# A head's retrieval in seven pieces behind seven gather steps, in place of four behind four

## The chip, the cores and the metric

One core of one Trainium2 chip runs the whole program in one launch. The metric is the device time in microseconds of one execution. Of three executions of the kernel before, the median is 2275.62 us (2271.41 to 2276.86).

## The reference, cut to what matters

One inference step of a decoder layer: 512 prompt tokens and 32 sample tokens, width 1024, float32. A mixer (a convolution branch, a dilated attention branch and gates) gives `x1`; then comes a lookup layer, PEER, with 16384 experts, and it is the lookup that the change is about:

```python
q = (hb @ w_peer_q).reshape(PEER_BLOCK, PEER_HEADS, 2, PEER_HALF)
s = jnp.einsum('thpc,hpkc->thpk', q, sub_keys)           # 8 heads x 2 halves x 128 scores
s1, i1 = lax.top_k(s[:, :, 0], PEER_TOPK)                # 16 best of each half
s2, i2 = lax.top_k(s[:, :, 1], PEER_TOPK)
cand = (s1[..., :, None] + s2[..., None, :])             # 16 x 16 sums
top_s, top_c = lax.top_k(cand, PEER_TOPK)                # 16 best sums
idx = e1 * N_KEYS + e2                                   # e1, e2: keys looked up in i1, i2 by top_c
g = softmax(top_s)
a = einsum(hb, expert_u[idx]);  out = (g * gelu(a)) @ expert_v[idx]
```

For each token and each of 8 heads, 16 experts are found ("the retrieval"), and one row of `expert_u` and one of `expert_v` is fetched for each.

## The kernel before, in words

**Tiles.** The tokens stand in five tiles: prompt tiles 0 to 3 (128 tokens each) and the sample tile, number 4 (`NT`, 32 tokens). The mixer runs in two passes, first over tiles 0, 1 and 4, then over 2 and 3.

**Gather steps.** The expert work is a row of 544 steps (`ST`), in the order of tiles 0, 1, 4, 2, 3. One step fetches 128 rows of 8 KB, u and v side by side, for 32 tokens and 4 of one head's 16 experts; a head of a prompt tile is 16 steps, a head of the sample tile 4. In each step:
- GpSimd issues the indirect DMA into one of six slots of `ring` (line 1088), after it has waited until the step six back has left its slot, and at a head's first step until the head's picks are there (`pick_ready`)
- VectorE waits for the rows and forms the 128 dot products with the tokens (line 1894; it will be called the dot)
- ScalarE applies Gelu (line 1480) and makes the weights `fold` (line 1483, from line 1476)
- TensorE multiplies them with the v halves into `acc` (line 1310) and with that frees the slot.

**The retrieval of a head** is VectorE's, but for three small things. Its four parts in the kernel before: `halves` (top 16 of both halves of the scores, by `top16`: MAX8, FIND_INDEX8, MATCH_REPLACE8, MAX8, FIND_INDEX8, lines 1794 to 1798), `candidates` (the 256 sums and their top 16, lines 1820 to 1826), `keys_named(q, 0)` (the first key of each of the 16, lines 1831 to 1837), and `experts` (the second key, then expert numbers and softmax weights, lines 1834 to 1847). ScalarE does the exponential (`head_exp`, line 1465), for which it waits until `candidates` is done; `experts` waits for it in turn. TensorE then spreads numbers and weights to 128 partitions (`spread`, line 1292), into the one bank `o` that the attention output (`O`) and the convolution (`C`) also use in turn; VectorE copies them out (`place`, lines 1859 and 1860). The scores of a head are loaded from memory by SyncE for tiles 0, 1 and 4 (`load_scores`, line 839) and are still on the chip for tiles 2 and 3.

**Where the retrieval stands.** `ITEMS` lists the 40 (tile, head) pairs by the step `at` at which each begins: a prompt head 16 steps ahead of its own first step, so at every 16th step, with the sample heads set between them, 8 steps off. `PARTS` sets part p of a head right behind the dot of step at + p, in VectorE's order. ScalarE does the exponential behind step at + 1.

**The order of everything.** A planner (`plan`) lays the mixer's work out in 508 ticks, and each engine goes through the same ticks in its own order: the tick's mixer tasks first, then gather steps up to `MARK[n]` (VectorE and ScalarE run 2 steps ahead of TensorE, GpSimd up to 6). The steps 0 to 271 are laid into the ticks of the second half of the mixer; after the last tick 272 steps are left, with nothing else beside them. This second stretch will be called the tail. `spread` and `place` stand in the second tick after the one in which VectorE passes step at + 3 (`place_picks`); in the tail `spread` stands ahead of step at + 5 of TensorE, and `place` behind the dot of step at + 7.

Of the kernel before, what the change touches and what calls it, by code (L numbers as in the profile page):

```python
# [9 lines left out]
ALU = mybir.AluOpType  # L10
# [19 lines left out]
KEYS, TOPK, PH, HALF = 128, 16, 8, 128  # L30
RMS_EPS, LN_EPS = 1e-6, 1e-5
NEG = -1.0e30
LOW = -3.0e38
# [63 lines left out]
def tile_rows(t):  # L97
    return P if t < NT else SMP
# [34 lines left out]
PH_OF = {t: p for p, some in enumerate(PAIRS) for t in some}  # L133
# [58 lines left out]
LEAD_V, LEAD_A = 2, 2  # L192
# [169 lines left out]
UNITS, TICKS, ENDS = plan()  # L362
# [32 lines left out]
START = ENDS["wq", 0, 0] + 8  # L395
# [26 lines left out]
MARK = step_marks()  # L422
# [12 lines left out]

ITEMS = item_list()
ITEM_NO = {(t, h): q for q, (_, t, h) in enumerate(ITEMS)}
PARTS = {}
for _q, (_at, _t, _h) in enumerate(ITEMS):
    for _p in range(4):  # L440
        if _at >= 0:
            PARTS.setdefault(_at + _p, []).append((_q, _p))
SCORES_AT = {ITEMS[q - 1][0] + 2 if q > 2 and (t, h) != (2, 0) else max(at - 3, 0): q for q, (at, t, h) in enumerate(ITEMS) if at >= 0}


def place_picks():

    tail = {}  # L450
    for q, (at, _, _) in enumerate(ITEMS):
        n = START if q == 0 else next((n for n in range(START, len(TICKS)) if MARK[n] + LEAD_V > at + 3), len(TICKS)) + 2
        if n < len(TICKS):
            TICKS[n].append(("P", q))
            TICKS[n].sort(key=lambda v: ORDER[v[0]])
        else:
            tail[at + 5] = q
    return tail


# [136 lines left out]
def program(nc, a, sc):  # L597
    with ExitStack() as ctx:
# [22 lines left out]
        tv, tif, caf, e12 = sb("tv", [P, 2, TOPK]), sb("tif", [P, 2, TOPK]), sb("caf", [P, 2, TOPK]), sb("e12", [P, 2, TOPK])  # L621
        ti, ca, ci = sb("ti", [P, 2, TOPK], U32), sb("ca", [P, 2, TOPK], U32), sb("ci", [P, TOPK], U32)
        cand, cv, ex = sb("cand", [P, TOPK, TOPK]), sb("cv", [P, TOPK]), sb("ex", [P, TOPK])
        nmx, exs = sb("nmx", [P, 1]), sb("exs", [P, 2])
# [39 lines left out]
        flat = ring[:, :, :].rearrange("p r d -> p (r d)")  # L664
# [43 lines left out]
        def kept_scores(t):  # L708

            return sx[:, 0:2 * PH * KEYS] if t == 2 else uT[:, :, :].rearrange("p c t -> p (c t)")[:, 0:2 * PH * KEYS]  # L710
# [750 lines left out]
        def _(eng):  # L1461
# [7 lines left out]
            def steps_upto(last):  # L1469
                for i in range(done[0], min(last, STEPS)):  # L1470
                    t, h, j, s = ST[i]
                    if j == J_ORDER[t][0] and s == 0:
                        eng.wait_ge(pick_ready, ITEM_NO[t, h] + 1)
                    if i >= 2:
                        eng.wait_ge(fold_ready, i - 1)
                    eng.activation(by_pick[:, i % 2, :], cst[:, C_FOLD:C_FOLD + SUB], ACT.Copy, scale=picks(i, 1)).then_inc(by_ready, 1)  # L1476
                    eng.wait_ge(dot_ready, i + 1)
                    if i >= 4:
                        eng.wait_ge(v_used, i - 3)
                    eng.activation(gel[:, i % 4:i % 4 + 1], dots[:, i % 4:i % 4 + 1], ACT.Gelu).then_inc(gel_ready, 1)  # L1480
                    eng.wait_ge(gel_ready, i + 1)
                    eng.wait_ge(by_ready, i + 1)
                    eng.activation(fold[:, i % 4, :], by_pick[:, i % 2, :], ACT.Copy, scale=gel[:, i % 4:i % 4 + 1]).then_inc(fold_ready, 1)  # L1483
                    for q, p in PARTS.get(i, ()):
                        if p == 1:
                            head_exp(q)
                done[0] = max(done[0], last)

# [8 lines left out]
            for n, tick in enumerate(TICKS):  # L1497
                if n == ENDS["glu", 0, 3]:
                    eng.wait_ge(rest_in, 16)
                for v in tick:  # L1500
                    if v[0] == "X0":
                        t = v[1]
# [10 lines left out]
                    elif v[0] == "XT":  # L1513
                        t, q = v[1:]
                        m = tile_rows(t)
# [236 lines left out]
        def _(eng):  # L1752
            count = [0]

            def link(ins):
                count[0] += 1
                ins.then_inc(chain, 1)
                eng.wait_ge(chain, count[0])

            def signal(ins, s, n):  # L1760
                ins.then_inc(s, 1)
                eng.wait_ge(s, n)
# [30 lines left out]
            def top16(values, index, x):  # L1793
                link(eng.max(values[:, 0:8], x))
                link(eng.max_index(index[:, 0:8], values[:, 0:8], x))  # L1795
                link(eng.match_replace(x, values[:, 0:8], x, LOW))
                link(eng.max(values[:, 8:16], x))  # L1797
                return eng.max_index(index[:, 8:16], values[:, 8:16], x)  # L1798

            def halves(q):  # L1800
                _, t, h = ITEMS[q]
                m, of = tile_rows(t), sco2
                if PH_OF[t]:
                    freed(eng, SB, s_free, ("SC", t, h // 2))
                    of = kept_scores(t)[:, 2 * KEYS * h:2 * KEYS * (h + 1)]
                elif q:
                    eng.wait_ge(sco_in, 16 * q)
                else:
                    freed(eng, SB, s_free, ("SC", 0, 0))
                    link(eng.tensor_copy(sco2[:, :], sco[:, 0, 0:2 * KEYS]))  # L1810
                for p in range(2):
                    ins = top16(tv[0:m, p, :], ti[0:m, p, :], of[0:m, KEYS * p:KEYS * (p + 1)])
                    if p:
                        signal(ins, half_done, q + 1)
                    else:
                        link(ins)

            def candidates(q):
                m = tile_rows(ITEMS[q][1])
                link(eng.tensor_copy(tif[0:m, :, :], ti[0:m, :, :]))  # L1820
                if q:
                    eng.wait_ge(o_ready, OB.no["P", q - 1] + 1)
                link(eng.tensor_tensor(cand[0:m, :, :], tv[0:m, 0, :].unsqueeze(2).to_broadcast([m, TOPK, TOPK]),
                                       tv[0:m, 1, :].unsqueeze(1).to_broadcast([m, TOPK, TOPK]), ALU.add))
                link(top16(cv[0:m, :], ci[0:m, :], cand[0:m, :, :].rearrange("p a b -> p (a b)")))
                signal(eng.tensor_scalar(nmx[0:m, :], cv[0:m, 0:1], -1.0, None, ALU.mult), top_ready, q + 1)

            def keys_named(q, p):
                m = tile_rows(ITEMS[q][1])
                if p == 0:  # L1830
                    link(eng.tensor_scalar(ca[0:m, 0, :], ci[0:m, :], 4, None, ALU.logical_shift_right))
                    link(eng.tensor_scalar(ca[0:m, 1, :], ci[0:m, :], TOPK - 1, None, ALU.bitwise_and))
                    link(eng.tensor_copy(caf[0:m, :, :], ca[0:m, :, :]))
                link(eng.tensor_tensor(cand[0:m, :, :], caf[0:m, p, :].unsqueeze(2).to_broadcast([m, TOPK, TOPK]),  # L1834
                                       cst[0:m, C_IOTA:C_IOTA + TOPK].unsqueeze(1).to_broadcast([m, TOPK, TOPK]), ALU.is_equal))
                link(eng.tensor_tensor(cand[0:m, :, :], cand[0:m, :, :], tif[0:m, p, :].unsqueeze(1).to_broadcast([m, TOPK, TOPK]), ALU.mult))  # L1836
                link(eng.tensor_reduce(e12[0:m, p, :], cand[0:m, :, :], AX, ALU.add))  # L1837

            def experts(q):
                m = tile_rows(ITEMS[q][1])  # L1840
                keys_named(q, 1)
                link(eng.scalar_tensor_tensor(out=e12[0:m, 0, :], in0=e12[0:m, 0, :], scalar=float(KEYS), in1=e12[0:m, 1, :], op0=ALU.mult, op1=ALU.add))
                own_j = cst[0:m, C_JM:C_JM + QUAD].unsqueeze(2).to_broadcast([m, QUAD, TOPK])
                link(eng.tensor_tensor(igm[0:m, :, 0, :], e12[0:m, 0:1, :].to_broadcast([m, QUAD, TOPK]), own_j, ALU.mult))
                eng.wait_ge(ex_ready, q + 1)
                link(eng.reciprocal(exs[0:m, 1:2], exs[0:m, 0:1]))
                signal(eng.scalar_tensor_tensor(out=igm[0:m, :, 1, :], in0=ex[0:m, :].unsqueeze(1).to_broadcast([m, QUAD, TOPK]), scalar=exs[0:m, 1:2], in1=own_j,
                                                op0=ALU.mult, op1=ALU.mult), ig_ready, q + 1)
# [12 lines left out]
                eng.sem_inc(o_free, 1)  # L1861

            def part(q, p):
                if p == 0:
                    halves(q)
                elif p == 1:
                    candidates(q)
                elif p == 2:
                    keys_named(q, 0)
                else:  # L1870
                    experts(q)

# [30 lines left out]
            for n, tick in enumerate(TICKS):  # L1903
# [182 lines left out]
                if n in CONV[0]:  # L2086
                    conv_upto(0, CONV[0][n])
                if START - 4 <= n < START:
                    part(0, n - START + 4)
                steps_upto(lead(n, LEAD_V))  # L2090
            steps_upto(STEPS)
            for f, (last, _, _) in enumerate(FIN):
# [65 lines left out]
```

## Time and profile before

| | |
|---|---|
| median of three runs | 2275.62 us |
| the profiled execution | 2276.75 us, span 2274.9 us |
| TensorE, VectorE, ScalarE, GpSimd busy | 71%, 65%, 38%, 33% of the span |
| indirect gathers | 544, 570.46 MB (1.049 MB each) |
| all DMA | 752.49 MB, mean 331 GB/s |
| VectorE: the dots | 544 x 1225 ns |
| GpSimd waiting for TensorE to free a slot | 878.1 us |

The span is cut into 40 slices of 56.9 us. The second half of the DMA row reads 9 in nearly every slice, the TensorE clock row falls from 9 to 5 in the 28th slice, where the mixer ends and the tail begins:

```profile
DVE  2587773114658687878887767336666765676774
PEclk9999999998899998789999999896555555555555
DMA  5333557666899989799999999999999999999998
```

A digit is a tenth of the slice's time (PEclk: of the full clock); 9 stands for 90% or more, so a 9 in the DMA row can still hide a few per cent.

### The profile page before, as it was taken

What the parts mean: (1) busy time and instruction counts of PE and PEld (TensorE: products, weight loads), DVE (VectorE), ACT (ScalarE), POOL (GpSimd) and SP (SyncE); (2) the same over time, 40 slices, a digit from 0 to 9 for tenths busy, and PEclk for the clock granted to TensorE, in tenths of its full rate; (3) what the DMA queues carried; (4) which work ended last, traced back from release to release, by engine and by line L of the source; (5) the groups of instructions that cost most, each with busy time, mean ns of one, the idle gap of its engine ahead of it and who ended that gap; (6) DMA issues with size and microseconds to landing.
All of it is one profiled execution on the core that took longest, in us unless ns stands there. A gap on an engine that the chain in (4) does not pass through costs nothing.

```text
span 2274.9 us, 33445 instructions
## 1 busy us (share of the span) xinstructions
PE 1614.9 (71%) x11548; PEld 737.8 (32%) x11548; DVE 1469.4 (65%) x3591; ACT 857.9 (38%) x2426; POOL 757.3 (33%) x713
## 2 busy tenths in 40 slices
PE   7999999996798877777778988794344343443343
PEld 3556655443343433434333433341000000000000
DVE  2587773114658687878887767336666765676774
ACT  2132243012445434544556543333333332333332
POOL 1254100001233243333533333333444343444343
PEclk9999999998899998789999999896555555555555
DMA  5333557666899989799999999999999999999998
GB/s 189 129 109 119 200 202 275 213 209 247 318 406 341 372 312 381 292 363 375 358 381 360 363 406 409 394 377 391 394 391 406 397 401 371 395 400 409 408 405 364
DMA packets 129188, 752.49 MB, mean 331 GB/s; under 512 B 16724, under 2 KB 40908, under 8 KB 51308
## 3 DMA queue, kind: packets, MB, share of 16 engines
q0 software_dynamic: 78336, 570.46, 63.7%
q1 hardware_dynamic: 50684, 179.90, 21.4%
q8 instruction: 92, 1.51, 0.3%
q14 instruction: 76, 0.62, 0.1%
HBM read 732.61 MB, written 18.54 MB: 330 GB/s over the span
## 4 chain that ended last, share of the span: by engine, by line
PE 34%; DMA 28%; DVE 24%; issue 9%; ACT 4%; POOL 1%; SPq 0%; DVEq 0%; POOLq 0%; ACTq 0%
DMA ring<-in_expert_uv,pick 25%; PE z L1156 20%; DVE ring L1894 6%; PE acc L1310 4%; PE z L1162 2%; PE o L1191 2%; DMA sx<-in_x_prompt 1%; DVE cand L1836 1%; DVE ti L1795 1%; DVE e L1837 1%; DVE ti L1798 1%; DVE cand L1834 1%; DVE tv L1797 1%; PE s L1181 1%; DVE tmp L1965 1%
## 5 line engine op out<-in xcount | busy, mean ns | idle before, releaser
L1088 POOL DMA_INDIRECT ring<-in_expert_uv,pick x544 | 624.2, 1147 | 967.0 <-PE acc L1310 878.1
L1894 DVE CUSTOM_DVE_ANT_0 ring<-ring,rep 128x1024 f32<-128x1024 f32 x544 | 660.2, 1225 | 375.8 <-DMA ring<-in_expert_uv,pick 346.4
L1310 PE MATMUL acc<-ring,fold 128*32 128x256 f32 x4352 | 461.3, 515 | 489.7 <-ACT fold L1483 487.2
L1156 PE MATMUL z<-wts,hT 128*128 128x384 f32 (+1 forms) x1408 | 611.5, 572 | 5.9 <-ACT hT L1492 3.1
L1480 ACT ACTIVATE gel<-dots 128x1 f32<-128x1 f32 x544 | 109.7, 202 | 782.9 <-DVE dots L1894 781.7
L1310 PEld LDWEIGHTS acc<-ring,fold 128*32 128x32 f32 x4352 | 105.9, 125 | 813.1 <-ACT fold L1483 745.6
L1156 PEld LDWEIGHTS z<-wts,hT 128*128 128x128 f32 x1408 | 259.5, 198 | 258.0 <-issue 193.4
L1156 PE MATMUL z<-wts,yT 128*128 128x512 f32 x384 | 195.3, 645 | 12.9 <-ACT yT L1492 6.2
L1483 ACT ACTIVATE fold<-by_pick,gel 128x32 f32<-128x32 f32 x544 | 174.8, 321 | 17.9
L1476 ACT ACTIVATE by_pick<-cst,pick 128x32 f32<-128x32 f32 x544 | 167.1, 307 | 0.0
L1787 DVE SCALAR_TENSOR_TENSOR yT<-uT,vec,yT 128x256 f32<-128x256 f32 x240 | 107.8, 501 | 2.3
L1156 PEld LDWEIGHTS z<-wts,yT 128*128 128x128 f32 x384 | 71.4, 201 | 101.5 <-issue 101.4
L1053 POOL TENSOR_SCALAR xss<-xss 128x1 f32<-128x1 f32 (+1 forms) x10 | 2.9, 289 | 283.5 <-ACT kvr L1688 224.2
L1480 ACT ACT_TABLE_LOAD x70 | 89.8, 1283 | 1.2
L1053 POOL TENSOR_SCALAR ssq<-ssq 128x6 f32<-128x6 f32 (+1 forms) x40 | 21.6, 540 | 174.7 <-DVE ssq L1949 173.9
L1191 PE MATMUL o<-kvr,pt 128*128 128x64 f32 x432 | 58.9, 294 | 16.0 <-ACT pt L1492 11.6
L1191 PEld LDWEIGHTS o<-kvr,pt 128*128 128x128 f32 x432 | 58.3, 211 | 26.4 <-ACT pt L1492 14.7
L1364 PE MATMUL t<-cst,sx 128*128 128x128 f32 x216 | 38.1, 295 | 36.6 <-ACT hoT L1492 20.2
L1981 DVE SCALAR_TENSOR_TENSOR sx<-s,cst 128x512 f32<-128x512 f32 (+3 forms) x72 | 36.8, 552 | 38.1 <-PE s L1181 36.1
L1054 POOL TENSOR_TENSOR ssq<-ssq,half_m 128x6 f32<-128x6 f32 (+1 forms) x40 | 53.4, 1336 | 3.5 <-POOL ssq L1053 0.2
L1628 ACT ACTIVATE sx<-sx,nm 128x384 f32<-128x384 f32 (+3 forms) x32 | 32.5, 1015 | 55.0 <-DVE nm L1992 54.8
L1492 ACT ACTIVATE pt<-t 128x512 f32<-128x512 f32 (+2 forms) x64 | 33.5, 523 | 50.7 <-PE t L1364 50.5
(250 smaller groups left out, 1715.5 us busy)
## 6 DMA issues: line engine op xcount, KB each, us to landing
wts<-in_w_qkv SPq DMA_DIRECT2D x24, 1536.0 KB, 7.7
wts<-in_w_glu SPq DMA_DIRECT2D x8, 2048.0 KB, 10.7
wts<-in_w_gate SPq DMA_DIRECT2D x8, 2048.0 KB, 12.7
wts<-in_w_wq SPq DMA_DIRECT2D x8, 2048.0 KB, 12.0
ring<-in_k_cache SPq DMA_DIRECT2D x16, 768.0 KB, 7.7
ring<-in_v_cache SPq DMA_DIRECT2D x16, 768.0 KB, 7.6
rep<-x_h SPq DMA_DIRECT2D x68, 128.0 KB, 9.2
ring<-in_expert_uv,pick POOLq DMA_INDIRECT x544, 11.4
```

Source lines behind the costliest of these rows:

```text
L1054: return eng.tensor_tensor(to, to, half_m[0:m, 0:w], ALU.pow)
L1088: eng.indirect_dma_start(ring[:, i % RING, :], None, a["expert_uv"], bass.IndirectOffsetOnAxis(picks(i, 0).bitcast(U32), 0)).then_inc(row_ ...
L1156: mm = eng.matmul(bank[:, 0:w], of[:, k, :], rows[:, k, :], start=(k == 0), stop=(k == depth - 1))
L1162: mm = eng.matmul(to, of[:, k, :], by, start=(k == 0), stop=(k == depth - 1))
L1191: mm = eng.matmul(ob[:, 0:HD], pt[:, P * j:P * (j + 1)], vv[:, hp % 2, u, P * g + HD * w:P * g + HD * (w + 1)], start=(j == 0), stop=(j == ...
L1310: mm = eng.matmul(acc[b][SUB * c:SUB * (c + 1), col:col + 256], fold[:, i % 4, :], ring[:, i % RING, D + 256 * c:D + 256 * (c + 1)], start ...
L1364: mm = eng.transpose(tpb[:, P * (j - 4 * q):P * (j - 4 * q + 1)], s_sb[:, XN[x] % 2, P * j:P * (j + 1)], ident)
L1476: eng.activation(by_pick[:, i % 2, :], cst[:, C_FOLD:C_FOLD + SUB], ACT.Copy, scale=picks(i, 1)).then_inc(by_ready, 1)
L1480: eng.activation(gel[:, i % 4:i % 4 + 1], dots[:, i % 4:i % 4 + 1], ACT.Gelu).then_inc(gel_ready, 1)
L1483: eng.activation(fold[:, i % 4, :], by_pick[:, i % 2, :], ACT.Copy, scale=gel[:, i % 4:i % 4 + 1]).then_inc(fold_ready, 1)
L1787: ins = eng.scalar_tensor_tensor(out=out, in0=src, scalar=cw[:, c, tap:tap + 1], in1=out, op0=ALU.mult, op1=ALU.add)
L1894: eng.tensor_tensor_reduce(u, u, rep[:, j, :], 1.0, 0.0, ALU.mult, ALU.add, dots[:, i % 4:i % 4 + 1]).then_inc(dot_ready, 1)
```

## The change

The retrieval's instructions stay the same, in the same order within a head. They are cut in seven pieces behind the dots of steps at to at + 6: first half's search, second half's search, the 256 sums and their best eight, the next eight and the negated maximum, the first key, the second key, the expert numbers and weights. The exponential stands behind step at + 4 of ScalarE, not at + 1. `spread` and `place` stand in the second tick after step at + 6 is passed; in the tail ahead of step at + 8 and behind the dot of step at + 10. The load of the next head's scores is issued one step later. Head 0, which is retrieved before the first step, keeps its four ticks, two pieces in each.

```diff
+PIECES = 7
 PARTS = {}
 for _q, (_at, _t, _h) in enumerate(ITEMS):
-    for _p in range(4):
+    for _p in range(PIECES):
         if _at >= 0:
             PARTS.setdefault(_at + _p, []).append((_q, _p))
-SCORES_AT = {ITEMS[q - 1][0] + 2 if q > 2 and (t, h) != (2, 0) else max(at - 3, 0): q for q, (at, t, h) in enumerate(ITEMS) if at >= 0}
+SCORES_AT = {ITEMS[q - 1][0] + 3 if q > 2 and (t, h) != (2, 0) else max(at - 3, 0): q for q, (at, t, h) in enumerate(ITEMS) if at >= 0}
...
-        n = START if q == 0 else next((n for n in range(START, len(TICKS)) if MARK[n] + LEAD_V > at + 3), len(TICKS)) + 2
+        n = START if q == 0 else next((n for n in range(START, len(TICKS)) if MARK[n] + LEAD_V > at + PIECES - 1), len(TICKS)) + 2
...
-            tail[at + 5] = q
+            tail[at + PIECES + 1] = q
...
-                        if p == 1:
+                        if p == 4:
                             head_exp(q)
...
+            def half_search(q, p):
+                m, of = scores_of(q, p)
+                ins = top16(tv[0:m, p, :], ti[0:m, p, :], of[0:m, KEYS * p:KEYS * (p + 1)])
+                if p:
+                    signal(ins, half_done, q + 1)
+                else:
+                    link(ins)
...
+            def candidates(q, p):
                 m = tile_rows(ITEMS[q][1])
+                flat = cand[0:m, :, :].rearrange("p a b -> p (a b)")
+                if p:
+                    link(eng.match_replace(flat, cv[0:m, 0:8], flat, LOW))
+                    link(eng.max(cv[0:m, 8:16], flat))
+                    link(eng.max_index(ci[0:m, 8:16], cv[0:m, 8:16], flat))
+                    signal(eng.tensor_scalar(nmx[0:m, :], cv[0:m, 0:1], -1.0, None, ALU.mult), top_ready, q + 1)
+                    return
                 link(eng.tensor_copy(tif[0:m, :, :], ti[0:m, :, :]))
...
-                link(top16(cv[0:m, :], ci[0:m, :], cand[0:m, :, :].rearrange("p a b -> p (a b)")))
-                signal(eng.tensor_scalar(nmx[0:m, :], cv[0:m, 0:1], -1.0, None, ALU.mult), top_ready, q + 1)
+                link(eng.max(cv[0:m, 0:8], flat))
+                link(eng.max_index(ci[0:m, 0:8], cv[0:m, 0:8], flat))
...
             def experts(q):
                 m = tile_rows(ITEMS[q][1])
-                keys_named(q, 1)
...
             def part(q, p):
-                if p == 0:
-                    halves(q)
-                elif p == 1:
-                    candidates(q)
-                elif p == 2:
-                    keys_named(q, 0)
+                if p < 2:
+                    half_search(q, p)
+                elif p < 4:
+                    candidates(q, p - 2)
+                elif p < 6:
+                    keys_named(q, p - 4)
                 else:
                     experts(q)
```

`scores_of` is the head of the old `halves`: it waits for the scores, and for the second half only names where they are.

## Rows read from the trace of the kernel before

**Rows 1.** VectorE's timeline, dots of the tail: start us, us, engine line operation [idle before]

```profile
1543.87 1.23 DVE L1894 CUSTOM_DVE_ANT_0 ring<-ring,rep 128x1024 f32<-128x1024 f32 x1 [1.25 <-DMA ring<-in_expert_uv,pick]
...
1584.86 1.23 DVE L1894 CUSTOM_DVE_ANT_0 ring<-ring,rep 128x1024 f32<-128x1024 f32 x1 [1.35 <-issue]
...
1632.70 1.23 DVE L1894 CUSTOM_DVE_ANT_0 ring<-ring,rep 128x1024 f32<-128x1024 f32 x1 [1.25 <-DMA ring<-in_expert_uv,pick]
...
1884.62 1.23 DVE L1894 CUSTOM_DVE_ANT_0 ring<-ring,rep 128x1024 f32<-128x1024 f32 x1 [1.26 <-DMA ring<-in_expert_uv,pick]
...
1982.71 1.22 DVE L1894 CUSTOM_DVE_ANT_0 ring<-ring,rep 128x1024 f32<-128x1024 f32 x1 [1.23 <-DMA ring<-in_expert_uv,pick]
...
2230.05 1.23 DVE L1894 CUSTOM_DVE_ANT_0 ring<-ring,rep 128x1024 f32<-128x1024 f32 x1 [1.22 <-DMA ring<-in_expert_uv,pick]
...
2267.73 1.23 DVE L1894 CUSTOM_DVE_ANT_0 ring<-ring,rep 128x1024 f32<-128x1024 f32 x1 [1.46 <-DMA ring<-in_expert_uv,pick]
```

**Rows 2.** The same timeline through one head's retrieval (tile 2, head 4)

```profile
1717.22 1.22 DVE L1894 CUSTOM_DVE_ANT_0 ring<-ring,rep 128x1024 f32<-128x1024 f32 x1 [1.23 <-DMA ring<-in_expert_uv,pick]
...
1720.21 0.29 DVE L1794 MAX8 tv<-sx 128x8 f32<-128x128 f32 x1
...
1722.05 1.23 DVE L1894 CUSTOM_DVE_ANT_0 ring<-ring,rep 128x1024 f32<-128x1024 f32 x1
...
1723.20 0.18 DVE L1820 CAST tif<-ti 128x32 f32<-128x32 uint32 x1
...
1724.87 0.09 DVE L1796 MATCH_VALUE_LOAD cand<-cv,cand 128x8 f32 x1
...
1726.57 1.22 DVE L1894 CUSTOM_DVE_ANT_0 ring<-ring,rep 128x1024 f32<-128x1024 f32 x1
...
1729.72 1.23 DVE L1894 CUSTOM_DVE_ANT_0 ring<-ring,rep 128x1024 f32<-128x1024 f32 x1
...
1732.24 0.17 DVE L1842 SCALAR_TENSOR_TENSOR e<-e 128x16 f32<-128x16 f32 x1
...
1733.27 1.23 DVE L1894 CUSTOM_DVE_ANT_0 ring<-ring,rep 128x1024 f32<-128x1024 f32 x1
```

**Rows 3.** GpSimd's timeline in the same head: a gather issued late

```profile
1730.49 1.27 POOL L1088 DMA_INDIRECT ring<-in_expert_uv,pick  x1 [4.24 <-PE acc L1310]
```

**Rows 4.** Busy time by engine, clock, DMA share, GB/s: a head begun at 2148.2

```profile
2148.20:2153.20 5.00, 1.60 (x16) 0.20 (x8) 4.61 (x19) 0.74 (x3) 2.20 (x2) 0.50 1.02 424
...
2163.20:2168.20 5.00, 2.53 (x32) 0.80 (x24) 4.83 (x12) 1.78 (x8) 1.57 (x2) 0.50 0.99 390
2168.20:2173.20 5.00, 3.96 (x36) 0.81 (x32) 3.50 (x8) 2.64 (x11) 3.78 (x5) 0.50 0.97 357
```

**Rows 5.** All gathers of line 1088, from issue to landing

```profile
DMA to landing us min/median/max: 5.5/11.4/21.9
```

**Rows 6.** Chain of waits in the tail: the landing that ends a head's stall

```profile
1778.93 6.82 DMA ring<-in_expert_uv,pick
```

**Rows 7.** ScalarE's timeline at the exponential of the head of rows 2

```profile
1726.57 0.31 ACT L1465 ACTIVATE ex<-cv,nmx 128x16 f32<-128x16 f32 x1 [1.40 <-DVE nmx L1826]
...
1727.20 1.28 ACT L1480 ACT_TABLE_LOAD   x1
1728.49 0.20 ACT L1480 ACTIVATE gel<-dots 128x1 f32<-128x1 f32 x1
```

**Rows 8.** Busy time of the engines, a stretch of the overlap and the tail

```profile
850.00:1150.00 300.00, 228.94 (x1428) 120.41 (x1426) 242.68 (x611) 155.01 (x388) 120.91 (x106) 0.87 0.94 356
...
1544.00:2230.00 686.00, 281.05 (x2212) 61.97 (x2211) 478.27 (x1187) 237.20 (x835) 296.40 (x257) 0.53 1.00 398
```

**Rows 9.** Chain of waits, 850 to 1150 us, share of the stretch by line

```profile
by line: DMA ring<-in_expert_uv,pick 21.1%; issue 13.7%; DVE ring L1894 10.6%; PE z L1156 4.7%; DVE nm L1991 3.5%; PE o L1191 3.5%; PE acc L1310 2.7%; DVE sx L1981 2.0%; DVE ti L1795 1.7%; DVE ti L1798 1.7%; DVE sco L1796 1.7%; PE t L1364 1
```

**Rows 10.** Line 1859, the first copy of `place`: what it waited for (us, times)

```profile
  PE o L1292: 26.3, 10
```

**Rows 11.** DMA issues: loads of a prompt head's scores, KB, median us to landing

```profile
sco<-x_sc SPq DMA_DIRECT2D x15, 128.0 KB, 12.2
```

More of the change, by code:

```diff
@@ L1798, in top16, with scores_of @@
                 return eng.max_index(index[:, 8:16], values[:, 8:16], x)
-            def halves(q):
+            def scores_of(q, p):
                 _, t, h = ITEMS[q]
                 m, of = tile_rows(t), sco2
+                if p:
+                    return m, kept_scores(t)[:, 2 * KEYS * h:2 * KEYS * (h + 1)] if PH_OF[t] else of
                 if PH_OF[t]:
@@ L1810, in halves @@
                     link(eng.tensor_copy(sco2[:, :], sco[:, 0, 0:2 * KEYS]))
[L1811 to L1818, printed above, removed]
-                m = tile_rows(ITEMS[q][1])
+                return m, of
+            def half_search(q, p):
[6 more added lines that the diff above has]
+            def candidates(q, p):
+                m = tile_rows(ITEMS[q][1])
+                flat = cand[0:m, :, :].rearrange("p a b -> p (a b)")
+                if p:
+                    link(eng.match_replace(flat, cv[0:m, 0:8], flat, LOW))
[3 more added lines that the diff above has]
+                    return
                 link(eng.tensor_copy(tif[0:m, :, :], ti[0:m, :, :]))
@@ L2088, in _ @@
                 if START - 4 <= n < START:
-                    part(0, n - START + 4)
+                    k = 2 * (n - START + 4)
+                    for p in range(k, min(k + 2, PIECES)):
+                        part(0, p)
                 steps_upto(lead(n, LEAD_V))
```

## The prediction, on record before the change was built

> **What bounds the kernel now.** First the two halves of the expert work are read apart. In the tail (1544 to 2230 us) the DMA share is 1.00 and TensorE is busy 281 of 686 us [rows 8]: the gathers bound it. In the overlap, of which 850 to 1150 us is typical, no engine is full (VectorE 243 of 300 us, TensorE 229, DMA share 0.94), and the clock granted is 0.87 [rows 8]; the reader is to see three resources near their end that take turns.
>
> Then the tail is read dot by dot. A dot with no retrieval near it waits 1.2 us for its rows [rows 1]. The last 15 steps, with no retrieval beside them, take 2267.73 - 2230.05 = 37.68 us, 2.51 us each: that is the pace of the gathers. The 256 steps before them take 2230.05 - 1543.87 = 686.2 us, 2.68 each [rows 1]. Held against 256 x 2.512 = 643.1 us, 43.1 us are lost, in 16 heads.
>
> Why a head loses time stands in its own rows. From its first dot on VectorE is behind: the dots start at 1717.22, 1722.05, 1726.57, 1729.72 and 1733.27 [rows 2]. Four steps take 16.05 us where the gathers need 4 x 2.51 = 10.04, so VectorE falls 6.0 us behind. A slot comes free only behind its dot, so GpSimd issues late, after 4.24 us of waiting for TensorE [rows 3]. A gather lands 11.4 us after issue in the median, 5.5 at best [rows 5], and 6.8 when it is waited for at the end of a stall [rows 6]: the queue holds 11.4 - 6.8 = 4.6 to 11.4 - 5.5 = 5.9 us of lead, less than 6.0. So it runs thin for a moment: 424 GB/s as the head begins, 390 and 357 some 15 and 20 us later [rows 4]. Those two stretches cost (34 + 67) / 424 x 5 us = 1.2 us.
>
> **The change part by part.** *The seven pieces.* Nothing is added or removed, so VectorE's total stays. The pieces are read off where they will be cut. A dot takes 1.15 us before the next operation (1722.05 to 1723.20). The two searches take 3.68 us together, cut at 1720.21, so 1.84 each; the sums and the best eight 1.67 (1723.20 to 1724.87), the rest 1.70; the first key 3.15 - 1.15 = 2.00; the second key 1732.24 - 1729.72 - 1.15 = 1.37; the numbers and weights 1.03 [rows 2]. With the dot, the seven steps take 2.99, 2.99, 2.82, 2.85, 3.15, 2.52 and 2.18 us. Against 2.51 each, VectorE is behind by 0.48, 0.96, 1.27, 1.61, 2.25, 2.26 and 1.93 us. Its worst is 2.3 in place of 6.0, under the lead of 4.6 to 5.9, so the queue should not run thin.
>
> *The exponential.* It brings two table loads of 1.28 us [rows 7]. Now ScalarE stands waiting for `candidates` while the first goes on (1.40 us of idle are left), and its Gelu of the next step comes at 1728.49, 0.7 us after the dot that it reads is done (1726.57 + 1.23). Behind step at + 4 the maximum is long there, but VectorE needs only 2.00 + 1.23 us to the end of the next dot, and ScalarE 0.65 (Gelu and `fold`) + 1.28 + 0.50 + 0.30 + 1.28 = 4.0: that Gelu is late by 0.7 to 0.8 us. The lateness of that slot is then 2.25 + 0.8 = 3.1 us, still under 4.6. The cost is 0; were the lead used up it would be 0.8 us a head, 31 us in 39 heads.
>
> The page "ScalarE: Activation LUTs" of the Trainium skill (section Table-load gate) puts such a load at about 2.7 us. The trace has 1.28 and decides. By the page's figure the Gelu would be 3.6 us late, the slot 5.9, and the tail would gain next to nothing: 2275.6 - 13 = 2263.
>
> *Picks later.* In the tail `place` moves from behind at + 7 to behind at + 10. The gather of the next head's first step, at + 16, needs the slot of at + 10, which comes free some 2 us after that dot (Gelu, `fold`, products), whereas the two copies of `place` follow the dot at once, 0.4 us. So the picks are there first, by 1.5 us. In the ticks, the planner's rule moves all 23 placements of heads 1 to 23 back, by one to five ticks; by the marks no `place` falls behind the dot of at + 10, so there too GpSimd finds the picks. The bank `o` is shared in order: in the old ticks 5 placements share a tick with an `O` or `C` or with the task that frees it, in the new ones 5 as well. VectorE waits 26.3 us in 10 `place`s now [rows 10]; I take no change, between -26 (all waits go) and +26 (as many again).
>
> *Scores.* The load is issued one step later and waits for the same place in the search, now one step later too. Behind it in SyncE's queue stand the weights, held no longer than before. Five steps of the overlap's 1009 / 272 = 3.7 us are 18.5 us, against 12.2 to landing [rows 11]: nothing.
>
> **The sum.** Tail: of the 43.1 us over the pace, three heads, which also reload tokens and store results, hold (47.84 + 98.09) - 3 x 40.19 = 25.4 [rows 1]. The other 13 hold 17.7, 1.36 each. The three are given the same 1.36; their other 21 us are traffic and stay. 16 x 1.36 = 21.8, less 0.15 a head for what may be left: 19.4 us gained. Bounds: 0 (the dips are the DMA's own) and 43 (all of it).
>
> Overlap: the half searches are on the chain that ended last. Three of their lines hold 5.1% of 300 us there, 15.3 us [rows 9]; the same share over 640 to 1150 us is 26 us. A lump cut in two lets the mixer's short tasks in between; I take half of it, 13 us gained. Bounds: 26 gained, and 26 lost at `place`. Above 1150 us TensorE and the DMA bound the overlap, and nothing is taken.
>
> 2276.75 - 19.4 - 13 = 2244.3 for an execution like the profiled one. The median of the runs is 1.1 us lower; the forecast is 2243.
>
> **The rivals.** (1) *Tail alone.* VectorE's total is the same, and at 243 of 300 us [rows 8] a lump cut in two may only shift the wait: 2275.6 - 19.4 = 2256. For it: overlap stalls change hands easily. Against: retrieval lines are on its chain.
>
> (2) *More in the overlap.* With dips gone, the overlap nears its DMA bound: 356 GB/s against the 424 that rows 4 show. Half of what its share of 0.94 leaves, over 510 us, is 15 more; with all 26 of the search: 2276 - 19 - 41 = 2215. Against: TensorE waits for much else there.
>
> (3) *Hidden anyway.* The lead is enough already and the dips are the DMA's. The Trainium skill's page "DMA: Bandwidth & Descriptors" (section Anatomy of one DMA) gives a transfer 2.0 us plus its bytes at 436 GB/s: 4.4 us for 1.049 MB, an estimate. By it the lead is 11.4 - 4.4 = 7.0 us, over 6.0, and the tail gains nothing. As a mechanism of rows, without that page: the lead would be over 6.0 us, the tail's term 0, the time 2263 with the overlap's gain, 2276 without. Against: the rate falls in the very slices in which the late gathers would be under way [rows 4], and the 15 steps without retrieval keep their pace.
>
> (4) *Slower: VectorE stands at a later `place`.* `place` is in VectorE's order and waits for `spread`, which waits in TensorE's order for the shared bank; every dot behind it stands too. Ten waits cost 2.6 us each [rows 10]. If all 23 placements in ticks waited so, 60 us, 34 more than now: 2276.75 + 34 - 19.4 = 2291, with no gain in the overlap. It decides from the point where the added waits pass 19.4 us, eight more. For it: they move among `O`s. Against: the distance from pieces to `spread` to `place` is still two ticks.
>
> **How the numbers follow.** Forecast 0.55, own range 2232 to 2256; rival 1 0.19; rival 2 0.12; rival 3 0.08; rival 4 0.06. 0.3% is 6.8 us, about what a measurement tells from no change. Faster takes the forecast, rivals 1 and 2 and a little of rival 3: 0.87; same most of rival 3: 0.07; slower 0.06. For 8 in 10 the range goes from 2212, past rival 2, to 2266, past rival 1 and the better case of rival 3: rival 3 without any gain and rival 4 are left out.
>
> **What would show it.** In a tail head the dots stand 2.8 to 3.2 us apart over five steps, none 4.5 or more; 16 steps take 40 to 40.5 us; GpSimd's longest wait falls under 3 us; 5 us stretches stay above 410 GB/s; ScalarE's idle time before the exponential is gone. Wrong: 41.5 us per 16 steps with the dots evenly spread, which is rival 3; `place` waiting over 45 us, which is rival 4.

## The result, and the profile after

The changed kernel takes 2248.93 us (median of 4 runs, 2247.53 to 2254.55) against 2273.51 us for the kernel before (4 runs, 2270.73 to 2276.86): a ratio of 0.9896, 95% interval 0.9872 to 0.992, 24.6 us less. The forecast was 2243, its range 2212 to 2266. The profiled execution has a span of 2245.8 us, 29.1 less than before's 2274.9.

The gain splits at step 272, in the same rows as before. VectorE's timeline, dots of the steps 0, 272, 288, 304, 528 and 543 (the dot is line 1907 in this kernel):

```profile
531.42 1.23 DVE L1907 CUSTOM_DVE_ANT_0 ring<-ring,rep 128x1024 f32<-128x1024 f32 x1 [7.17 <-DMA ring<-in_expert_uv,pick]
...
1529.19 1.23 DVE L1907 CUSTOM_DVE_ANT_0 ring<-ring,rep 128x1024 f32<-128x1024 f32 x1 [1.26 <-DMA ring<-in_expert_uv,pick]
...
1569.78 1.23 DVE L1907 CUSTOM_DVE_ANT_0 ring<-ring,rep 128x1024 f32<-128x1024 f32 x1 [1.34 <-issue]
...
1615.98 1.23 DVE L1907 CUSTOM_DVE_ANT_0 ring<-ring,rep 128x1024 f32<-128x1024 f32 x1 [1.25 <-DMA ring<-in_expert_uv,pick]
...
2201.10 1.22 DVE L1907 CUSTOM_DVE_ANT_0 ring<-ring,rep 128x1024 f32<-128x1024 f32 x1 [1.25 <-DMA ring<-in_expert_uv,pick]
...
2238.58 1.23 DVE L1907 CUSTOM_DVE_ANT_0 ring<-ring,rep 128x1024 f32<-128x1024 f32 x1 [1.47 <-DMA ring<-in_expert_uv,pick]
```

The tail takes 2201.10 - 1529.19 = 671.9 us, where it took 686.2 [rows 1]: 14.3 less. The 15 steps after it keep their pace (37.48 us, before 37.68). The overlap, step 0 to 272, takes 997.8 us; before it was 1543.87 - 534.88 = 1009.0, from this first dot:

```profile
534.88 1.23 DVE L1894 CUSTOM_DVE_ANT_0 ring<-ring,rep 128x1024 f32<-128x1024 f32 x1 [7.18 <-DMA ring<-in_expert_uv,pick]
```

So the overlap gives 11.2. Step 0 begins 3.5 us earlier; in the kernels of this study it begins anywhere from 529.6 to 536.1, so that part is scatter.

The overlap's gain falls late. From step 0 to step 160 the kernel before takes 610.6 us and the changed one 606.5; from step 160 to 272 they take 398.4 and 391.3. The busy table of this second part (columns as in [rows 4]), before:

```profile
1145.45:1543.87 398.42, 337.21 (x1734) 146.97 (x1731) 255.08 (x621) 178.94 (x473) 132.71 (x118) 0.92 0.98 384
```

and after:

```profile
1137.93:1529.19 391.26, 333.08 (x1734) 143.96 (x1730) 254.35 (x620) 177.80 (x472) 136.35 (x118) 0.93 1.00 393
```

The DMA share is 0.98 there before and 1.00 after. The engines of the DMA were busy as long in both (0.98 x 398.4 = 390 us, 1.00 x 391.3 = 391), so the time gained is time in which they stood idle.

The same head as in [rows 2], dot by dot:

```profile
1697.42 1.23 DVE L1907 CUSTOM_DVE_ANT_0 ring<-ring,rep 128x1024 f32<-128x1024 f32 x1 [1.24 <-DMA ring<-in_expert_uv,pick]
...
1700.41 1.23 DVE L1907 CUSTOM_DVE_ANT_0 ring<-ring,rep 128x1024 f32<-128x1024 f32 x1
...
1703.40 1.23 DVE L1907 CUSTOM_DVE_ANT_0 ring<-ring,rep 128x1024 f32<-128x1024 f32 x1
...
1706.21 1.23 DVE L1907 CUSTOM_DVE_ANT_0 ring<-ring,rep 128x1024 f32<-128x1024 f32 x1
...
1709.06 1.22 DVE L1907 CUSTOM_DVE_ANT_0 ring<-ring,rep 128x1024 f32<-128x1024 f32 x1
...
1712.21 1.23 DVE L1907 CUSTOM_DVE_ANT_0 ring<-ring,rep 128x1024 f32<-128x1024 f32 x1
```

The dots stand 2.99, 2.99, 2.81, 2.85 and 3.15 us apart, and the next two 2.52 and 2.19, to 0.01 us what was worked out. What that does to the gathers is seen in 5 us stretches of a head (columns as in [rows 4], the same head, now begun at 2119.67):

```profile
2134.67:2139.67 5.00, 1.89 (x16) 0.40 (x16) 4.76 (x12) 3.15 (x10) 2.77 (x2) 0.50 1.01 413
2139.67:2144.67 5.00, 2.54 (x28) 0.79 (x24) 3.21 (x6) 1.86 (x8) 2.80 (x3) 0.50 1.01 421
```

Where 390 and 357 GB/s stood, 413 and 421 stand, and no stretch of the eight of this head is under 413. Beside the pieces of the head of [rows 3] GpSimd's longest wait is 1.87 us, where it was 4.24:

```profile
1716.11 0.94 POOL L1089 DMA_INDIRECT ring<-in_expert_uv,pick  x1 [1.87 <-PE acc L1311]
```

ScalarE's timeline at the exponential of the head of [rows 7]:

```profile
1712.20 0.31 ACT L1466 ACTIVATE ex<-cv,nmx 128x16 f32<-128x16 f32 x1
...
1714.12 0.20 ACT L1481 ACTIVATE gel<-dots 128x1 f32<-128x1 f32 x1
```

It no longer waits for the maximum, and its Gelu comes 0.68 us after the dot it reads (1712.21 + 1.23), as forecast. In the busy table the overlap's stretch of [rows 8] gains nothing (348 GB/s, before 356), while the tail's rate is up from 398 to 408 GB/s:

```profile
850.00:1150.00 300.00, 226.16 (x1386) 119.03 (x1386) 241.45 (x606) 158.91 (x394) 121.59 (x104) 0.85 0.91 348
...
1529.00:2201.00 672.00, 286.91 (x2212) 62.75 (x2212) 477.59 (x1187) 237.07 (x836) 336.68 (x257) 0.51 1.01 408
```

### The profile page after: what moved, and what is told of

Read it like the earlier page. It is cut to its first block, busy times and chain, and to the rows that moved or that the text cites. A ratio compares the mean times of both kernels' runs of the same rounds, so it can differ in the third digit from the quotient of the medians.

```text
span 2245.8 us, 33467 instructions
## 1 busy us (share of the span) xinstructions
PE 1616.8 (72%) x11548; PEld 736.5 (33%) x11548; DVE 1466.2 (65%) x3591; ACT 857.2 (38%) x2426; POOL 805.0 (36%) x713
## 4 chain that ended last, share of the span: by engine, by line
DMA 32%; PE 32%; DVE 22%; issue 7%; ACT 5%; POOL 1%; SPq 0%; DVEq 0%; ACTq 0%; POOLq 0%
DMA ring<-in_expert_uv,pick 30%; PE z L1157 19%; DVE ring L1907 8%; PE acc L1311 4%; PE z L1163 2%; DMA sx<-in_x_prompt 1%; PE o L1192 1%; PE t L1365 1%; DVE tmp L1978 1%; ACT fold L1484 1%; DVE ti L1796 1%; ACT gel L1481 1%; DVE ti L1799 1%; DVE tmp L1971 1%; DVE nm L2004 1%
## 5 line engine op out<-in xcount | busy, mean ns | idle before, releaser
L1089 POOL DMA_INDIRECT ring<-in_expert_uv,pick x544 | 674.0, 1239 | 899.0 <-PE acc L1311 829.3
L1311 PE MATMUL acc<-ring,fold 128*32 128x256 f32 x4352 | 470.4, 524 | 458.4 <-ACT fold L1484 458.1
L1629 ACT ACTIVATE sx<-sx,nm 128x384 f32<-128x384 f32 (+3 forms) x32 | 32.5, 1015 | 50.5 <-DVE nm L2005 50.3
```

The source lines that it names most:

```text
L1089: eng.indirect_dma_start(ring[:, i % RING, :], None, a["expert_uv"], bass.IndirectOffsetOnAxis(picks(i, 0).bitcast(U32), 0)).then_inc(row_ ...
L1311: mm = eng.matmul(acc[b][SUB * c:SUB * (c + 1), col:col + 256], fold[:, i % 4, :], ring[:, i % RING, D + 256 * c:D + 256 * (c + 1)], start ...
```

## The experiments

Most kernels cut the overlap's 24 heads and the tail's 16 differently. They are the changed kernel with this edit, and differ in the lists, in `EXP_AT` (the step, counted from at, behind which the exponential stands, in the overlap and in the tail) and, in one, in the ticks of the picks:

```diff
+FIRST_CUT, TAIL_CUT = ...        # pieces joined behind one dot, e.g. [[0, 1], [2, 3], [4], [5, 6]]
+def cut(q):
+    return TAIL_CUT if ITEMS[q][1] in (2, 3) else FIRST_CUT
...
-    for _p in range(PIECES):
+    for _p in range(len(cut(_q))):
...
-        n = START if q == 0 else next((n for n in range(START, len(TICKS)) if MARK[n] + LEAD_V > at + PIECES - 1), len(TICKS)) + 2
+        n = START if q == 0 else next((n for n in range(START, len(TICKS)) if MARK[n] + LEAD_V > at + len(cut(q)) - 1), len(TICKS)) + 2
...
-            tail[at + PIECES + 1] = q
+            tail[at + len(cut(q)) + 1] = q
...
-                        if p == 4:
+                        if p == EXP_AT[ITEMS[q][1] in (2, 3)]:
...
-                    for q, p in PARTS.get(i, ()):
-                        part(q, p)
+                    for q, k in PARTS.get(i, ()):
+                        for p in cut(q)[k]:
+                            part(q, p)
```

The ticks of `spread` and `place` follow the last piece, so they move with the number of pieces. Each kernel's tail and overlap are read from one execution, its ratio from all runs.

**Half of the change each: t7 and o7.** In t7 `FIRST_CUT` is the old `[[0, 1], [2, 3], [4], [5, 6]]` with the exponential behind at + 1, and the tail has seven pieces; o7 the other way round.

> Seven pieces for the 16 heads of tiles 2 and 3 (the tail), the old four for the 24 heads before. Theory (lead): the tail loses its thin queue and nothing else changes; tail (first dot of step 272 to that of step 528) 672 us as with seven pieces everywhere, against 686 before; the overlap (steps 0 to 272) 1009 us as before; time 14 us under before, 2259. Rival (the whole is one chain, the gain in the overlap is what shifts the tail): time within 4 us of before or of the full change.

> Seven pieces for the 24 heads of the overlap, the old four in the tail. Theory (lumps): the overlap is shorter by 8 to 15 us than before, the tail 686 us as before; time 2260 to 2266. Rival (the overlap's gain was one execution's chance, or a wait that only moves): time within 3 us of before, about 2273.

Measured, t7: 2259.3 us, ratio 0.9939 (0.9918 to 0.996). Steps 272 and 528:

```profile
1537.66 1.23 DVE L1915 CUSTOM_DVE_ANT_0 ring<-ring,rep 128x1024 f32<-128x1024 f32 x1 [1.25 <-DMA ring<-in_expert_uv,pick]
...
2209.09 1.23 DVE L1915 CUSTOM_DVE_ANT_0 ring<-ring,rep 128x1024 f32<-128x1024 f32 x1 [1.24 <-DMA ring<-in_expert_uv,pick]
```

o7: 2263.89 us, ratio 0.9962 (0.9944 to 0.998). Steps 0, 272 and 528:

```profile
530.41 1.23 DVE L1915 CUSTOM_DVE_ANT_0 ring<-ring,rep 128x1024 f32<-128x1024 f32 x1 [7.13 <-DMA ring<-in_expert_uv,pick]
...
1528.70 1.23 DVE L1915 CUSTOM_DVE_ANT_0 ring<-ring,rep 128x1024 f32<-128x1024 f32 x1 [1.25 <-DMA ring<-in_expert_uv,pick]
...
2216.69 1.22 DVE L1915 CUSTOM_DVE_ANT_0 ring<-ring,rep 128x1024 f32<-128x1024 f32 x1 [1.25 <-DMA ring<-in_expert_uv,pick]
```

t7's tail is 671.4 us, o7's 688.0, and o7's overlap is 998.3. The two halves take 14.2 and 9.7 us off the before of the same chip (2273.55); together 23.9, the whole change 24.6. They are two separate gains, and both are real. The tail is steady from kernel to kernel: 670.5 to 671.9 us in the six with seven pieces and six slots, 686.2 and 688.0 in the two with four.

**How far behind VectorE may be: tail2 and tail5.** `TAIL_CUT` is `[[0, 1, 2, 3], [4, 5, 6]]` (exponential behind at) or `[[0], [1], [2, 3], [4], [5, 6]]` (behind at + 3).

> Overlap as in the change; in the tail two pieces: both searches and the candidates behind step at, the keys and numbers behind at + 1. VectorE is then 8.7 us behind after two steps, against 6.0 with four pieces and 2.3 with seven. Theory (lead of 4.6 to 5.9 us in the gather queue): each head loses about 2.7 us more than with four pieces, so the tail is 672 + 16 x (0.9 + 2.7) = 730 us and the time 2307. Rival (only the total of VectorE's work counts, or the dips are the DMA's own): tail 672 to 686, time 2249 to 2263.

> Overlap as in the change; in the tail five pieces: only the two searches are parted (behind at and at + 1), the rest as in the four pieces, one step later. VectorE is 4.65 us behind at worst. Theory (lead of 4.6 to 5.9 us): at the lower end of the lead, so nearly all is gained, tail 672 to 676 us, time 2249 to 2253. Rival (loss in proportion to the lag, no threshold): 0.9 x (4.65 - 2.3) / (6.0 - 2.3) = 0.57 us a head, tail 681, time 2258.

Measured, tail2: 2297.97 us, ratio 1.0099 (1.0069 to 1.013), steps 272 and 528:

```profile
1531.74 1.23 DVE L1915 CUSTOM_DVE_ANT_0 ring<-ring,rep 128x1024 f32<-128x1024 f32 x1 [1.26 <-DMA ring<-in_expert_uv,pick]
...
2249.57 1.23 DVE L1915 CUSTOM_DVE_ANT_0 ring<-ring,rep 128x1024 f32<-128x1024 f32 x1 [1.25 <-DMA ring<-in_expert_uv,pick]
```

tail5: 2249.33 us, ratio 0.9896 (0.987 to 0.9922), steps 272 and 528:

```profile
1524.90 1.22 DVE L1915 CUSTOM_DVE_ANT_0 ring<-ring,rep 128x1024 f32<-128x1024 f32 x1 [1.26 <-DMA ring<-in_expert_uv,pick]
...
2197.19 1.22 DVE L1915 CUSTOM_DVE_ANT_0 ring<-ring,rep 128x1024 f32<-128x1024 f32 x1 [1.25 <-DMA ring<-in_expert_uv,pick]
```

The tails are 717.8 and 672.3 us. A lag of 4.65 us costs no more than one of 2.3; 6.0 costs 0.9 us a head, 8.7 costs 2.9. There is a threshold, so it is a lead that is used up and neither VectorE's total nor the DMA's own doing. In the tail, parting the two searches would have done, with the exponential one step behind the maximum.

**Taking a slot away: ring5_4 and ring5_7.** The kernel before and the changed one, both with

```diff
-RING = 6
+RING = 5
...
-        ring = sb("ring", [P, RING, 2 * D])
+        ring = sb("ring", [P, 6, 2 * D])
```

> Kernel before, but the steps use five of the six slots of ring, so one gather fewer is under way. Theory (lead): the lead falls by one step, 2.5 us, to 2.1 to 3.4; the lag of 6.0 us with four pieces is 2.6 to 3.9 over it, against 0.1 to 1.4 now, so a tail head loses about 2.5 us more than in the kernel before: tail 686 + 40 = 726 us. The dots without retrieval beside them stay 2.49 apart (steps 528 to 543 in 37.5 us). Rival (the dips are the DMA's own, or a fixed cost of a head): tail 686 as before. In the overlap GpSimd has a slot less; loss there open.

> The change, with five of the six slots of ring. Theory (lead): lag 2.3, with the late exponential 3.1, against a lead of 2.1 to 3.4: at the edge, tail 672 to 690 us, so 36 us or more under the four pieces with five slots; splitting is worth more where the lead is smaller. Rival (a fixed cost of a head): the same 14 us apart as with six slots.

Measured: 2361.68 us (ratio to before 1.0401, 1.0381 to 1.0422) and 2304.92 (1.0141, 1.0122 to 1.0159). Steps 272 and 528 of ring5_4:

```profile
1594.33 1.23 DVE L1894 CUSTOM_DVE_ANT_0 ring<-ring,rep 128x1024 f32<-128x1024 f32 x1 [1.25 <-DMA ring<-in_expert_uv,pick]
...
2312.56 1.23 DVE L1894 CUSTOM_DVE_ANT_0 ring<-ring,rep 128x1024 f32<-128x1024 f32 x1 [1.25 <-DMA ring<-in_expert_uv,pick]
```

and of ring5_7:

```profile
1579.55 1.22 DVE L1907 CUSTOM_DVE_ANT_0 ring<-ring,rep 128x1024 f32<-128x1024 f32 x1 [1.24 <-DMA ring<-in_expert_uv,pick]
...
2258.20 1.23 DVE L1907 CUSTOM_DVE_ANT_0 ring<-ring,rep 128x1024 f32<-128x1024 f32 x1 [1.24 <-DMA ring<-in_expert_uv,pick]
```

The tails are 718.2 and 678.7 us, 39.6 apart in place of 14.3. The retrieval is the same as with six slots; one slot less makes its lumps nearly three times as dear. The lead is the slots'. The rest of the loss is the overlap's, which the expectation left open: with five slots it takes 1063.5 and 1048.9 us, with six 1009.0 and 997.8.

**The floor: notail.** Only the last piece of a tail head is kept, and it recomputes nothing:

```diff
-        if _at >= 0:
+        if _at >= 0 and (_t not in (2, 3) or _p == PIECES - 1):
...
+                if ITEMS[q][1] in (2, 3):
+                    link(eng.tensor_copy(igm[0:m, 0:1, 1, :], igm[0:m, 0:1, 1, :]))
+                    eng.sem_inc(ig_ready, 1)
+                    return
```

> The change without the retrieval of the 16 heads of the tail: searches, candidates, keys and exponential are left out, the numbers and weights spread are stale ones, so the output is not the reference's; gathers, dots, products and the placing of picks stay. It gives the tail's floor. Theory: seven pieces leave nothing of the retrieval on the tail, tail 668 to 672 us, 16 steps about 40.5 with a single late landing of 1 us in most. Rival (the 0.9 us that 16 steps hold over 16 x 2.487 is retrieval's): tail 655 to 658, 39.8 in 16 steps.

There is one run: 2240.81 us. Steps 272 and 528:

```profile
1529.01 1.23 DVE L1911 CUSTOM_DVE_ANT_0 ring<-ring,rep 128x1024 f32<-128x1024 f32 x1 [1.26 <-DMA ring<-in_expert_uv,pick]
...
2193.88 1.23 DVE L1911 CUSTOM_DVE_ANT_0 ring<-ring,rep 128x1024 f32<-128x1024 f32 x1 [1.26 <-DMA ring<-in_expert_uv,pick]
```

The tail is 664.9 us, between the two expectations. So of the 21.3 us that the whole retrieval cost the tail before, the seven pieces take 14.3 and leave 7.0, some 0.4 a head.

**The exponential left where it was: exp1tail.**

```diff
-                        if p == 4:
+                        if p == (1 if ITEMS[q][1] in (2, 3) else 4):
```

> The change, but in the tail the exponential stays behind step at + 1 on ScalarE, as in the kernel before; it then waits for the maximum that VectorE has only behind the dot of at + 3. ScalarE's Gelu of at + 2 comes some 6.4 us after its dot, and that slot is free 7.4 us late. Theory (lead of 4.6 to 5.9 us): each tail head loses 1.5 to 2.8 us, tail 672 + 16 x 2.1 = 706 us, time 2283: the change's gain in the tail hangs on the exponential's move. Rival (ScalarE's place does not matter, VectorE's lumps alone do): tail 672, time 2249.

Measured: 2281.61 us, ratio 1.0052 (1.0027 to 1.0077). Steps 272 and 528:

```profile
1529.94 1.23 DVE L1907 CUSTOM_DVE_ANT_0 ring<-ring,rep 128x1024 f32<-128x1024 f32 x1 [1.26 <-DMA ring<-in_expert_uv,pick]
...
2231.52 1.23 DVE L1907 CUSTOM_DVE_ANT_0 ring<-ring,rep 128x1024 f32<-128x1024 f32 x1 [1.26 <-DMA ring<-in_expert_uv,pick]
```

The tail is 701.6 us, 29.7 more than with the exponential behind at + 4, and 15.4 more than in the kernel before: without the move on ScalarE the pieces lose in the tail about what they gain with it. Its waits in the tail (1540 to 2260 us; in all, times, longest) name the stand, 5.8 us a head:

```profile
ACT ex L1466 <- DVE nmx L1832: 92.4, 16, 7.9
```

**What the overlap gains from: x4e, o5, o6, x4p.** All have the change's tail. x4e: four pieces in the overlap, the exponential behind at + 2. o5: five, only the searches parted. o6: six, `[[0, 1], [2], [3], [4], [5], [6]]`, only the searches together.

> Tail as in the change; in the overlap the old four pieces, but the exponential one step later, behind at + 2. With four pieces ScalarE waits some 28 us in the overlap for the maximum; here that wait should be gone. Theory 1 (lumps of VectorE): overlap as with four pieces, about 1007 us, time 2259 as with seven pieces in the tail alone. Theory 2 (ScalarE standing for the maximum holds the mixer's evictions): overlap near 998, time 2249 to 2252.

> Tail as in the change; in the overlap five pieces, only the two searches parted, exponential behind at + 3. Theory 1 (the halves of the search are the lump that counts): all of the overlap's gain, time 2249 to 2251. Theory 2 (ScalarE's wait): the same, since the exponential is past the maximum here too. Rival (every lump counts by its size): half of it, time 2254.

> Tail as in the change; in the overlap six pieces: the two searches in one, all else parted as in the change, exponential behind at + 3. Theory 1 (the search's lump): the overlap's gain is gone, time 2257 to 2259. Theory 2 (ScalarE's wait): the gain is kept, time 2249 to 2251. Rival (every lump by its size): in between, 2254.

Measured: 2258.66 us (0.9934, 0.9921 to 0.9948), 2265.33 (0.9959, 0.9945 to 0.9972) and 2250.12 (0.9901, 0.9886 to 0.9916). ScalarE's wait for the maximum, 21.2 us in t7's overlap, is gone in x4e and nothing is won by it: its overlap is 1006.2 us, t7's 1005.6. Steps 0 and 272 of x4e:

```profile
536.10 1.22 DVE L1915 CUSTOM_DVE_ANT_0 ring<-ring,rep 128x1024 f32<-128x1024 f32 x1 [7.21 <-DMA ring<-in_expert_uv,pick]
...
1542.28 1.23 DVE L1915 CUSTOM_DVE_ANT_0 ring<-ring,rep 128x1024 f32<-128x1024 f32 x1 [1.25 <-DMA ring<-in_expert_uv,pick]
```

Parting the searches alone makes the overlap longer than it was; o6, with the searches in one lump, has the whole gain (998.3):

```profile
531.43 1.23 DVE L1915 CUSTOM_DVE_ANT_0 ring<-ring,rep 128x1024 f32<-128x1024 f32 x1 [6.82 <-DMA ring<-in_expert_uv,pick]
...
1529.74 1.23 DVE L1915 CUSTOM_DVE_ANT_0 ring<-ring,rep 128x1024 f32<-128x1024 f32 x1 [1.26 <-DMA ring<-in_expert_uv,pick]
```

Steps 0 and 272 of o5, 1020.8 us apart in the profiled execution, which was the slowest of its five (2271.07 us):

```profile
532.76 1.23 DVE L1915 CUSTOM_DVE_ANT_0 ring<-ring,rep 128x1024 f32<-128x1024 f32 x1 [6.83 <-DMA ring<-in_expert_uv,pick]
...
1553.56 1.23 DVE L1915 CUSTOM_DVE_ANT_0 ring<-ring,rep 128x1024 f32<-128x1024 f32 x1 [1.26 <-DMA ring<-in_expert_uv,pick]
```

With the number of pieces the picks' ticks move too, so x4p moves them alone: x4e with

```diff
-        n = START if q == 0 else next((n for n in range(START, len(TICKS)) if MARK[n] + LEAD_V > at + len(cut(q)) - 1), len(TICKS)) + 2
+        n = START if q == 0 else next((n for n in range(START, len(TICKS)) if MARK[n] + LEAD_V > at + PIECES - 1), len(TICKS)) + 2
```

> Tail as in the change; in the overlap the old four pieces with the exponential behind at + 2, but spread and place in the ticks that the change gives them. It tells the later picks from the cut. Theory P (which ticks the shared bank is taken in decides the overlap): overlap near 998 us as with six and seven pieces, time 2249 to 2252. Theory C (the cut of candidates, keys and numbers decides): overlap 1006 us as in the same kernel with the old ticks, time 2258 to 2260. In between: both.

Measured: 2278.67 us against 2276.37 for before beside it, ratio 1.0006 (0.9989 to 1.0024). Steps 0 and 272, 1029.3 us apart:

```profile
533.26 1.23 DVE L1915 CUSTOM_DVE_ANT_0 ring<-ring,rep 128x1024 f32<-128x1024 f32 x1 [6.79 <-DMA ring<-in_expert_uv,pick]
...
1562.55 1.23 DVE L1915 CUSTOM_DVE_ANT_0 ring<-ring,rep 128x1024 f32<-128x1024 f32 x1 [1.25 <-DMA ring<-in_expert_uv,pick]
```

Both theories missed: with the old cut the later picks make the overlap 23 us longer than x4e's. They are no gain, they are a price; the change, which has them too, is 31 us under x4p there, so the cut pays it back with interest. The medians say the same with smaller numbers: measured against before on each chip, and with the tail's gain taken off, x4e's overlap is 0.6 us over before's, o5's 7.5 and x4p's 18, while o6's is 8 under and the change's 10. Two waits between VectorE and TensorE go with the later or earlier ticks, both of the picks: `place` waiting for `spread`, and `spread` for the last operation of the retrieval. From step 0 to 272 (in all, times, longest), in the kernel before:

```profile
DVE pick L1859 <- PE o L1292: 25.4, 9, 7.8
...
PE o L1292 <- DVE cand L1847: 16.8, 7, 7.8
```

in the changed kernel:

```profile
DVE pick L1872 <- PE o L1293: 17.5, 8, 5.0
...
PE o L1293 <- DVE cand L1860: 13.6, 5, 5.3
```

in o5:

```profile
PE o L1301 <- DVE cand L1868: 33.9, 7, 8.6
...
DVE pick L1880 <- PE o L1301: 17.4, 10, 5.5
```

and in x4p, where the second is not met at all:

```profile
DVE pick L1880 <- PE o L1301: 44.6, 14, 9.3
```

The sums are 42, 31, 51 and 45 us, the overlaps 1009, 998, 1021 and 1029. Too early a tick for the pieces, and TensorE stands; too late a one, and VectorE does. The two long overlaps have the larger sums and the change the smallest, but the waits account for a part only: 9 of o5's 12 us over before, 2 of x4p's 20. And they are not where the change gains. Up to step 160 its sum is 10.6 us under before's (21.9 against 32.5) and its time 4.1 us; behind step 160 the sums are alike (9.2 and 9.7) and the time is 7.1 us less.

The time behind step 160 tells the kernels apart: 385 to 392 us in the six with the change's overlap (after, o7, tail2, tail5, exp1tail, notail), 390 in o6, 397 to 398 in before, t7 and x4e, 406 in o5, 409 in x4p. Up to step 160 the six take 606 to 615 us and the three with the old pieces 608 to 611, so nothing is shown to be gained there. That the lead is at work behind step 160, as in the tail, would fit: by the pieces' lengths VectorE is 3.6 us behind at worst in o6 and 4.65 in o5, both under the tail's threshold, and o5 then loses its gain at the hand-over of the picks. No run tests it alone, and what decides the overlap stays open. No kernel of the study is faster than the change; tail5 and o6 equal it.

## Why the prediction was right, point by point

**The pace, the lag and the lead** were right. The pieces' lengths came out to 0.01 us a step, the place of the threshold between 4.65 and 6.0 is that of the rows (4.6 to 5.9), and it moves with the slots. The signs were met, one only just missed: 16 steps were to take 40 to 40.5 us and take 40.7 in most plain heads, and GpSimd's longest wait, to be under 3 us, is 2.7 in the plain heads behind the first (in the first, where the mixer ends, 8.1). All tails can be put on one line, fitted to these runs: a head costs about 0.73 us for each us that its latest slot lies beyond 4.8, or, with one slot and so 2.5 us of lead less, beyond 2.3. For tail2 (8.7) that is 2.8, measured (717.8 - 671.9) / 16 = 2.9; exp1tail (7.4) 1.9 and 1.9; before (6.0) 0.9 and 0.9; ring5_4 (6.0) 2.7 and 2.9; ring5_7 (3.1) 0.6 and 0.4. Why the slope is not 1 isn't shown.

**The tail's term was 19.4 and is 14.3.** The mechanism held, the size did not, in two places. The 13 plain heads were to give 1.36 - 0.15 each and gave 1.00: the pace of 40.19 us per 16 steps, read from the last 15, is the floor (notail has 40.18 in its plain heads), but with retrieval they stay at 40.55. That the last 15 steps gave the floor is partly luck: they take 37.45 to 38.49 us in the kernels with six slots, so 39.9 to 41.1 per 16. And the three heads with other traffic were given the same, but gave 1.2 us in all: 46.20 against 47.84 in the first, none in the other two. Those two hold 96.2 to 99.3 us together in every kernel of the study, tail2 (99.3) and ring5_4 (98.9) among them, whose plain heads lose most. So there VectorE's lumps cost little; it seems that where reloads slow the landings anyway, they are waited out beside them.

**The overlap's term was 13 and is 11.2 in the profiled execution, 9.7 by o7's median. Its reason was wrong, and so was its place; that the number came near is luck.** "A lump cut in two lets the mixer's short tasks in between" was taken from the search's share of the chain; o6 keeps the search whole and has the gain, o5 cuts it alone and loses 12 us (7.5 by the medians). The gain was put between 640 and 1150 us, and nothing above, because TensorE and the DMA bound the overlap there. Above is where it lies: 7.1 of the 11.2 us come behind step 160, at 1145 us, and the 4.1 before it are within the scatter. Where the DMA binds, the time in which it stands idle can still be won. A line's share of the chain does not say what cutting it gives, when the cut also moves what comes behind it.

**The exponential at no cost** was right, and exp1tail shows that the move was needed for the pieces to pay at all.

**Picks later: no change** was half right. In the tail no gather waits for picks. In the ticks `place` waits 18.2 us in all, not 26.3 [rows 10]:

```profile
  PE o L1293: 18.2, 9
```

But the later ticks cost 23 us with the old cut (17 by the medians), so they are not neutral; rival 4 is a real mechanism (44.6 us of waiting at `place` in x4p), and it did not come to bear only because the cut was made finer with it.

**The other rivals.** Rival 1, the tail alone, is t7: 2259, where 2256 was given. Rival 2, 2215, fell as a number: the DMA share of the stretch from 850 to 1150 us is 0.91, before 0.94. Its mechanism is seen only behind step 160, where the rate goes from 384 to 393 GB/s. Rival 3 fell: a lag of 6.0 us costs 0.9 us a head. By the Trainium skill's page "DMA: Bandwidth & Descriptors" (section Anatomy of one DMA) a lag of 6.0 would be hidden, since 1.049 MB would take 4.4 us, an estimate from its figures. The trace does not agree, the shortest landing in the changed kernel is 5.6 us:

```profile
DMA to landing us min/median/max: 5.6/11.6/21.5
```

The sum, 32.4, was 8 us high against the medians' 24.6: five by the tail's term, three by the overlap's.

## What to carry to other kernels

Where a ring of buffers feeds an engine that also does other work, hold the longest time that the engine falls behind against the ring's lead. The rows put it between the median landing less that of a stalled gather (11.4 - 6.8 = 4.6 us) and the median less the shortest (5.9); the fit, 4.8, is at the lower end. In the tail of this kernel lumps below it cost next to nothing, and above it each us cost 0.73 us, each time. Cut only until the lag is under the lead, and move what waits for a piece on another engine with it. In a written-out order of several engines, moving work and moving its hand-over are two changes: try each alone before either is called the reason.

## What the runs showed of the hardware that was not expected

A DMA share of 0.97 or 0.99 does not mean a full rate: it stood so at 357 and 390 GB/s [rows 4], where 1.02 stood at 424. The rate fell by 16% and 8% while the share fell by 5% and 3%, so the rate shows the thin queue far better.

A tail head of the changed kernel takes 40.55 us in the mean of the 13 plain ones, most of them 40.7 and two 39.71, where 16 steps of 2.49 are 39.8: one landing comes about 1 us late in most heads. Without retrieval (notail, one run) the mean is 40.18. What is late there isn't settled.
